# Two transformer blocks in split fp32 on one core: value projections in 512 columns, one modulation batch divided, and the head of the second block's layers reordered

## The reference

```python
for i in range(2):                                    # first block
    sh1, sc1, g1, sh2, sc2, g2 = split(silu_c @ ada_w[i] + ada_b[i], 6)
    h, hc = rmsnorm(x) * (1 + sc1) + sh1, rmsnorm(xc) * (1 + csc1) + csh1
    q, k, v = split(concat(h, hc) @ wqkv, 3)          # i = 0: differential attention, 8 heads
    x = x + g1 * (attend(q, k, v) @ wo)               # i = 1: neighbourhood attention, 16 heads
    x = x + g2 * (gated(conv(norm_mod(x, sc2, sh2) @ w_up)) @ w_down)
for l in range(2):                                    # second block
    p = rmsnorm(x) @ w_in                             # q, kv, gates, fox q/k/v, fox f, ...
    kc, vc = compress(k_c), compress(v_c)             # flat @ w1, silu, @ w2
    logf = log_sigmoid(fox_f + bias); c = cumsum(logf)
    x = x + merged(nsa, pool, conv, fox) @ w_out
```

## Time and profile before

| what | value |
|---|---|
| median of three runs | 1661.72 us (1661.22 to 1662.11) |
| profiled execution | 1660.64 us, its span 1658.5 us |
| TensorE busy, share of the span | 1606.6 us, 97% |
| VectorE, ScalarE, GpSimd busy | 54%, 45%, 33% |
| mean granted TensorE clock | 0.987 |

### The profile page before, as it was taken

One profiled execution on the slowest core, in us unless ns is written; L12 is line 12 of the kernel. 1 busy time (PEld: TensorE's weight loads), 2 busy tenths in 40 slices (PEclk: granted clock), 3 DMA queues, 4 the chain that ended last, 5 costly groups with the idle time before them and its releaser, 6 DMA issues.

```text
span 1658.5 us, 26678 instructions
## 1 busy us (share of the span) xinstructions
PE 1606.6 (97%) x10956; PEld 1404.6 (85%) x10956; DVE 890.6 (54%) x1406; ACT 749.2 (45%) x1359; POOL 545.7 (33%) x358
## 2 busy tenths in 40 slices
PE   7999988999999999999999999998999999999998
PEld 4779557778767888778968999998999999899998
DVE  4334584455524554342265888548575457668434
ACT  5223584444313443243375655445544444554443
POOL 2214253322202222121172111024423577423554
PEclk9999999999999999999999999999999999999999
DMA  9264601443255222357224454554435545533551
GB/s 395 82 254 156 229 1 52 153 155 143 86 187 187 94 78 79 136 203 230 99 54 155 148 184 155 175 174 147 161 123 174 179 149 172 178 128 127 178 195 60
DMA packets 52984, 249.39 MB, mean 150 GB/s; under 512 B 20608, under 2 KB 21760, under 8 KB 26368
## 3 DMA queue, kind: packets, MB, share of 16 engines
q1 hardware_dynamic: 44400, 244.42, 42.4%
q10 hardware_dynamic: 8464, 3.28, 1.0%
HBM read 246.63 MB, written 1.05 MB: 149 GB/s over the span
## 4 chain that ended last, share of the span: by engine, by line
PE 86%; DVE 6%; ACT 3%; issue 1%; DMA 1%; POOL 1%; ACTq 1%; SPq 0%; POOLq 0%; DVEq 0%
PE psq L528 17%; PE psq L529 17%; PE psq L530 17%; PE ps L528 6%; PE ps L529 6%; PE ps L530 6%; PE ps L541 2%; PE psq L883 2%; PE psq L884 1%; PE psq L885 1%; DVE WL L510 1%; PE ps L1304 1%; PE psq L2122 1%; PE ps L1293 1%; PE psq L1261 1%
## 5 line engine op out<-in xcount | busy, mean ns | idle before, releaser
L528 PE MATMUL psq<-NH,WH 128*128 128x256 f32 (+1 forms) x1640 | 519.8, 317 | 3.9 <-DVE NL L793 2.0
L510 DVE TENSOR_TENSOR WL<-RAW,WH 128x1024 fp32r<-128x1024 f32 (+3 forms) x264 | 320.2, 1237 | 368.4 <-ACT WH L500 368.2
L529 PE MATMUL psq<-NL,WH 128*128 128x256 f32 (+1 forms) x1640 | 513.4, 313 | 0.0
L530 PE MATMUL psq<-NH,WL 128*128 128x256 f32 (+1 forms) x1640 | 513.3, 313 | 0.0
L510 POOL TENSOR_TENSOR WL<-RAW,WH 128x1024 fp32r<-128x1024 f32 (+2 forms) x116 | 302.3, 2608 | 556.2 <-ACT WH L500 543.8
L500 ACT ACTIVATE WH<-RAW 128x1024 fp32r<-128x1024 f32 (+2 forms) x380 | 361.0, 1000 | 177.7 <-DMA RAW<-wstream 127.2
L528 PEld LDWEIGHTS psq<-NH,WH 128*128 128x128 f32 x1640 | 314.2, 192 | 33.4 <-issue 12.0
L530 PEld LDWEIGHTS psq<-NH,WL 128*128 128x128 f32 x1640 | 314.1, 192 | 18.1
L529 PEld LDWEIGHTS psq<-NL,WH 128*128 128x128 f32 x1640 | 314.3, 192 | 16.8
L528 PE MATMUL ps<-NH,WH 128*128 128x256 f32 (+1 forms) x376 | 124.6, 331 | 0.0
L529 PE MATMUL ps<-NL,WH 128*128 128x256 f32 (+1 forms) x376 | 123.5, 328 | 0.0
(11 more groups left out here) (349 smaller groups left out, 2845.8 us busy)
## 6 DMA issues: line engine op xcount, KB each, us to landing
RAW<-wstream SPq DMA_DIRECT2D x196, 1024.0 KB, 4.9
RAW<-wstream SPq DMA_DIRECT2D x32, 704.0 KB, 4.1
K<-first SPq DMA_DIRECT2D x4, 1024.0 KB, 16.7
X<-xin SPq DMA_DIRECT2D x2, 1024.0 KB, 6.2
V<-first SPq DMA_DIRECT2D x2, 1024.0 KB, 19.2
Q<-first SPq DMA_DIRECT2D x2, 1024.0 KB, 24.9
BR<-rpb ACTq DMA_DIRECT2D x8, 256.0 KB, 10.0
BR<-rpb SPq DMA_DIRECT2D x8, 256.0 KB, 8.5
```

The costliest lines, as they stand in the source:

```text
L510: e.tensor_tensor(WL[:, u % 3, a:z], RAW[:, v % 3, a:z], WH[:, u % 3, a:z].bitcast(F32), ALU.subtract).then_inc(w_lo_p if pool else w_lo_v, 1)
L528: e.matmul(o, lh, rh, start=start, stop=False)
L529: e.matmul(o, lh, rl, start=False, stop=False)
L530: return e.matmul(o, ll, rh, start=False, stop=stop)
```

## The change

1. The values are projected in two pairs of units, each unit four input tiles by 512 columns (`pe_values`): 12 matmuls of 512 columns for each of four token tiles, each token tile in a bank of its own; the sums of a pair stay in their four banks (0 to 3, then 4 to 7) over both units. ScalarE copies four banks after the second unit of each pair. The waits move with it: token tiles 0 and 2 of the first unit wait for the copies of the last query and key units, `pe_diff` waits for all V copies before `pe_ada(2, 0)`.
2. Batch 5 keeps parameter 4 alone, with four units of two input tiles by 1024 columns; parameter 5 becomes batch 6, whose units are loaded behind `up(1,0)` and `up(1,1)` and multiplied in `pe_wo` (two) and ahead of the first two `up` units (two) of layer 1, its transposes ahead of the sixth. `dve_ada_halves` adds the two partial sums. The split of `up(1,1)` comes behind the norm.
3. `pe_out_turn` runs at the end of its step, behind the score product.
4. In the head `vf` is projected right behind `kf`, the LF transposes run between the two `cmp` products; ScalarE splits `vf` and the first `cmp` unit ahead of the forget gate, and VectorE makes the low parts of `vf` and `FHL`, both rotations, the low part of the first `cmp` unit and `dve_out_gain` ahead of the LF additions.

The core of the diff (bookkeeping of the orders, shapes and weight packing, and renumbered waits are left out):

```diff
 UP_ADA = {("up", 0, 0): (0, 1, 2, 3), ("up", 0, 2): (4,), ("up", 0, 3): (5,), ("up", 0, 4): (6,), ("up", 0, 5): (7,)}
-QKV_ADA = {("qkv", 1, 4): (0, 1, 2, 3), ("qkv", 1, 6): (4,), ("qkv", 1, 7): (5,), ("qkv", 1, 0): (6,), ("qkv", 1, 1): (7,)}
+QKV_ADA = {("qkv", 1, 4): (0, 1, 2, 3)}
+LATE_ADA = {("up", 1, 0): (0, 1, 2), ("up", 1, 1): (3,)}
+def ada_units(b):
+    return 8 if b < 5 else 4
...
             for j in range(4):
-                mm = e.matmul(AB[32 * j:32 * j + 32, :], CB[:, k, :], RAW[:, v % 3, 512 * j:512 * j + 512],
-                              start=k == 0, stop=k == DT - 1)
+                c = k if b < 5 else 2 * k + j // 2
+                mm = e.matmul(AB[32 * j:32 * j + 32, :], CB[:, c, :], RAW[:, v % 3, 512 * j:512 * j + 512],
+                              start=k == 0, stop=k == ada_units(b) - 1)
...
         def act_ada_row(e, b):
-            e.wait_ge(gemm, product(("ada", b, DT - 1)))
+            e.wait_ge(gemm, product(("ada", b, ada_units(b) - 1)))
...
+        def dve_ada_halves(e, b):
+            t = 32 + 8 * (b - 5)
+            to = ADA[:, 1, t:t + 8, :].rearrange("p (c q) v -> p c q v", c=2)
+            part = AB[:, :].rearrange("p (q k c s) -> p k c q s", q=4, k=2, c=2)
+            bias = small_at("adab", 48 + t, 8).rearrange("p (c q) -> p c q", c=2).unsqueeze(3)
+            e.wait_ge(ada_fin, b)
+            e.tensor_tensor(to, part[:, 0, :, :, 0:2], bias.to_broadcast([P, 2, 4, 2]), ALU.add).then_inc(ada_half, 1)
+            e.wait_ge(ada_half, b - 4)
+            e.tensor_tensor(to, part[:, 1, :, :, 0:2], to, ALU.add).then_inc(ada_par, 1)
         def dve_ada(e, b):
+            if b >= 5:
+                dve_ada_halves(e, b)
+                return
...
             for i in range(4):
-                b = qk_slot(8 + i)
...
                     pe_ada_turn(e, 1)
-                if i < 3:
-                    e.wait_ge(qk_sb, qk_outputs_before(l, 8 + i - 2))
-                else:
-                    pe_last_values(e, l)
-                    continue
-                pe_tall(e, ("qkv", l, 8 + i), [bank[b], bank[b + 1]], 256, nothing)
+                pe_values(e, l, i)
+        def pe_values(e, l, i):
+            key, pr, kh = ("qkv", l, 8 + i), i // 2, i % 2
+            v, wh, wl = weights(key)
+            for t in range(4):
+                if i == 3:
+                    (pe_na_qk if l else pe_diff_qk)(e, t)
+                if i == 0 and t % 2 == 0:
+                    e.wait_ge(qk_sb, qk_outputs_before(l, 7 + t // 2))
+                if i == 2 and t == 3:
+                    e.wait_ge(ada_par, 5 if l else 1)
+                c = slice(t * P, t * P + P)
+                for k in range(4):
+                    if t == 0:
+                        wait_weights(e, v, k)
+                    kk = 4 * kh + k
+                    mm = mm3(e, bank[4 * pr + t], NH[:, kk, c], NL[:, kk, c], wh[:, k, :], wl[:, k, :], kk == 0, kk == 7)
+                if kh or t == 3:
+                    mm.then_inc(gemm, 1)
...
                 key = ("qkv", l, 8 + i)
-                b = qk_slot(8 + i)
-                for q in range(2):
-                    if i == 3:
-                        (act_na_exp if l else act_diff_exp)(e, q)
-                    e.wait_ge(gemm, product(key, q))
-                    e.activation(V[l][:, 2 * q:2 * q + 2, 256 * i:256 * i + 256], pair(bank[b + q]),
+                for t in range(4 if i % 2 else 0):
+                    if i == 3 and t < 2:
+                        (act_na_exp if l else act_diff_exp)(e, t)
+                    e.wait_ge(gemm, product(key, t))
+                    e.activation(V[l][:, t, 256 * (i - 1):256 * (i - 1) + 512], bank[4 * (i // 2) + t],
...
                     h, qt, k0, nk = diff_job(j)
-                    if age == 11 and qt == 3 and h < 7:
-                        pe_out_turn(e, h)
...
                         pe_diff_qk(e, j)
+                j = n - 11
+                if 0 <= j < 28 and diff_job(j)[1] == 3:
+                    pe_out_turn(e, j // 4)
+                if n == 2:
+                    e.wait_ge(v_sb, 8)
...
                     e.wait_ge(att_pt, PT1 + 2 * p + 2)
+                    if p == 0:
+                        e.wait_ge(v_sb, 16)
...
                         pe_sums(e, n, m)
-            if l == 0:
-                pe_ada(e, 3, 0)
+            pe_ada(e, 6 if l else 3, 0)
...
                 pe_ada(e, 3, 2)
+            else:
+                pe_ada(e, 6, 1)
...
             for i in range(4):
-                split_hi(e, ahead(("wo", l, i)))
+                if (l, i) != (1, 3):
+                    split_hi(e, ahead(("wo", l, i)))
...
                         pe_ada_turn(e, 4)
+                    if l == 1 and j < 2:
+                        pe_ada(e, 6, 2 + j)
+                    if l == 1 and j == 6:
+                        pe_ada_turn(e, 6)
...
                         dve_ada(e, 3 + c)
+                    if l == 1 and jj == 6:
+                        dve_ada(e, 6)
...
             pe_raw_head(e, l)
-            for name in ("vn", "qf", "kf"):
+            for name in ("vn", "qf", "kf", "vf"):
                 pe_proj(e, l, name)
-            e.wait_ge(fx_v, FXV * l + 7)
-            for q in range(2):
-                mm = e.transpose(bank[3][:, q * P:q * P + P], LF[:, q, :], IDENT)
-            mm.then_inc(fx_tr, 1)
-            pe_proj(e, l, "vf")
...
             act_plain(e, l, "vn", VN[:, :, :])
+            act_plain(e, l, "qf", QF[:, :, :], 0.125)
+            for kind in range(2):
+                if kind == 0:
+                    e.wait_ge(flat, 5 * l + 5)
+                f = FLT[:, kind, :].rearrange("p (k n) -> p k n", k=16)
+                e.activation(FHV[:, kind, :, 0, :], f, ACT.Copy).then_inc(flat_hi, 1)
+            split_hi(e, ahead(unit_key(l, "kf")))
...
             e.activation(GS, VN[:, :, 128:140], ACT.Tanh, scale=0.5).then_inc(gs_a, 1)
-            act_plain(e, l, "qf", QF[:, :, :], 0.125)
-            for kind in range(2):
-                if kind == 0:
-                    e.wait_ge(flat, 5 * l + 5)
-                f = FLT[:, kind, :].rearrange("p (k n) -> p k n", k=16)
-                e.activation(FHV[:, kind, :, 0, :], f, ACT.Copy).then_inc(flat_hi, 1)
-            act_plain(e, l, "kf", KF[:, :, :])
+            act_out_of(e, l, "kf", KF[:, :, :])
+            act_plain(e, l, "vf", VF[:, :, :])
+        def act_decay(e, l):
...
                              bias=const_at("rows", 3 * a + 2)).then_inc(fx_a, 1)
-            act_plain(e, l, "vf", VF[:, :, :])
...
             e.memset(LF[:, :, :].bitcast(U32), 0).then_inc(fx_v, 1)
+            lo_prep(e, l, "qf", False)
             dve_turn(e, l, 0, QN[:, :, :])
+            for kind in range(2):
+                f = FLT[:, kind, :].rearrange("p (k n) -> p k n", k=16)
+                e.wait_ge(flat_hi, 2 * l + kind + 1)
+                e.tensor_tensor(FHV[:, kind, :, 1, :], f, FHV[:, kind, :, 0, :].bitcast(F32),
+                                ALU.subtract).then_inc(flat_lo, 1)
+            e.memset(CM[:, 0:384].bitcast(U32), 0).then_inc(cm_zero, 1)
+            dve_turn(e, l, 1, KN[:, :, :])
+            lo_prep(e, l, "kf", False)
+            if l == 0:
+                dve_out_gain(e, 5, "nout")
...
             e.tensor_scalar(GS, GS, 0.5, 0.5, ALU.mult, ALU.add).then_inc(gs_v, 1)
-            for kind in range(2):
-                f = FLT[:, kind, :].rearrange("p (k n) -> p k n", k=16)
-                e.wait_ge(flat_hi, 2 * l + kind + 1)
-                e.tensor_tensor(FHV[:, kind, :, 1, :], f, FHV[:, kind, :, 0, :].bitcast(F32),
-                                ALU.subtract).then_inc(flat_lo, 1)
-            e.memset(CM[:, 0:384].bitcast(U32), 0).then_inc(cm_zero, 1)
-            lo_prep(e, l, "qf", False)
-            dve_turn(e, l, 1, KN[:, :, :])
-            lo_prep(e, l, "kf", False)
-            if l == 0:
-                dve_out_gain(e, 5, "nout")
+            lo_prep(e, l, "vf", False)
+        def dve_decay(e, l):
...
                 mm.then_inc(gemm, 1)
+                if kind == 0:
+                    e.wait_ge(fx_v, FXV * l + 7)
+                    for q in range(2):
+                        mm = e.transpose(bank[3][:, q * P:q * P + P], LF[:, q, :], IDENT)
+                    mm.then_inc(fx_tr, 1)
...
                              ACT.Copy).then_inc(sb_copy, 1)
+                if kind == 0:
+                    act_decay(e, l)
...
                 split_lo(e, ahead(("cmp", l, kind)), pool)
+                if not pool and kind == 0:
+                    dve_decay(e, l)
```

More of the change, by code:

```diff
@@ L189, in unit_orders @@
         add(("qkv", 1, i), 1000)
[L190 to L195, removed]
+        if i == 5:
+            for k in range(ada_units(5)):
+                add_ada(5, k)
     for i in range(8, 12):
@@ L201, in unit_orders @@
         add(("up", 1, j), 1000)
+        for k in {0: (0, 1, 2), 1: (3,)}.get(j, ()):
+            add_ada(6, k)
     for m in range(DT):
@@ L222, in unit_orders @@
```

(36 more changed lines are left out.)

11 lines of the change are left out of this document (5 added, 6 removed).

## The result

The changed kernel takes 1646.54 us (median of four runs, 1643.65 to 1651.31) against 1661.47 for the kernel before (four runs): ratio 0.9918, interval 0.9889 to 0.9947. It is faster by 14.9 us where 23.8 were forecast; the time lies inside the range, near the case "the heads hand their wait on" (1646). The profiled execution is the longest of the four, 1651.31 us, span 1649.2.

A forecast was written before the change was run, and what follows sets the result against it. The prediction took TensorE's matmul stream as the bound, busy 1606.6 of 1658.5 us. Its terms summed to -23.8 against 1660.64, giving 1636.8, or 1637.9 with the median 1.1 above; range from 1632 with 2 us for the value stage's bounds to 1648.

The forecast's parts named there:

- the heads hand their wait on: Rival: in the hybrid heads vf's wait moves to cmp, FHL or the gain, half of 17.0 left: 1646; chance 0.16.
- Value projections: Value stages of both layers: 192 matmuls of 512 columns replace 384 of 256, 2.4 us less a layer.
- The wait in layer 0: Layer 0 value stage: third token tile of unit 8 waits 2.5 us for key copies, plus 1.5 for the clock.
- The last V copy: Ahead of pe_ada(2, 0): TensorE waits for the last V copy, +0.5 us (0 to 0.7).
- The output turn: Differential attention loop: the turn's wait of 1.20 goes but is given back through VectorE's scaling, -0.2 us (0 to -6.0).
- Batch 5: Layer 1: query and key stage -5.8 us from four units and a bias hole gone; ahead of the feed-forward net -0.5.
- The head of hybrid layer 0: Next projection starts 8.9 us earlier despite a 0.9 cmp hole, and 1.9 less for low clock: -10.8 us.
- the clock falls behind the cmp hole: Hybrid layer 0's head: +3.2 us, within the rival of new holes and the clock, 1642, chance 0.20.
- The head of hybrid layer 1: vf starts without its wait, and transposes and cmp end at 1430.75 instead of 1436.95: -6.2 us.
- The signs of being wrong: Layer 0's head: next projection starting later than 14 us behind vf; or the value stage showing a clock under 1.
- The value stage on four banks: Rival: cycling four banks drops the clock to 1.2 GHz, 1665 at 140 matmuls; nearly all of slower's 0.04 chance.
- the case with a low-clock stretch left: Head of hybrid layer 0: alternative to the -10.8 us if a low-clock stretch remains, given as -7.6.

The follow-up runs named there:

- the mended kernel: Changed kernel with last key unit's copies ahead of the split, low half of kf ahead of the flattening, both rotations behind everything else: 1631.53 us, again 1632.02.
- copies first: Changed kernel with ScalarE copying layer 0's last key unit out before the split that waits for a weight load: 1643.33 us.
- the old values: Value projections as before, four units of 256 columns, all else as in the kernel of 1631.53 us: 1637.55 us.
- the old turn: Output turn ahead of the score product again, all else as in the kernel of 1631.53 us: 1633.28 us.
- the second rotation alone: Changed kernel with only VectorE's second rotation in the hybrid heads moved behind everything else: 1636.14 us.
- the low half of kf alone: Changed kernel with only VectorE's low half of kf moved ahead of the flattening in the hybrid heads: 1654.94 us.

## Why the prediction was partly right

*Value projections.* Right. Layer 1 gained 2.7 (2.4 forecast), layer 0 without its new hole 2.36. The Trainium skill's fixed 2.5 ns a matmul (TensorE: Matmul & The Clock Gate, section "Wait — 56ns, not 53.3ns?") doesn't account for it: by it a layer would have gained 0.5, and undoing this part alone cost 5.5 us, of which the low clock in that profile explains some 1.7.

*The wait in layer 0.* Right in place and size: 2.35 for 2.5, released by the copy that was named, and gone when ScalarE's order is turned. The 1.5 for the clock behind it was there in one profile and not in the other.

*The last V copy.* Right: 0.69 us at `pe_ada(2, 0)`.

*The output turn.* Right: a little, a period of 9.97 instead of 10.06, and by the path that was named. VectorE's scaling waits 1.31 us for the turn, and the maximum behind it begins 2.1 us after the score product (238.10 against 236.01), where 2.0 was forecast. The score product now waits where the turn did (0.64 and 0.35 of the next period), for ScalarE:

```profile
236.01 1.13 PE L1123 MATMUL psq<-K,Q 64*128 64x512 f32 x4 [0.64 <-ACT PP L1174]
237.07 0.66 PE L1103 MATMUL ps<-CONST,TMP 128*128 128x128 f32 x4
...
241.02 0.70 PE L1123 MATMUL psq<-K,Q 64*128 64x512 f32 x2 [0.35 <-ACT TMP L1174]
```

```profile
237.83 0.35 DVE L1228 TENSOR_SCALAR TMP<-ps,STAT 128x128 f32<-128x128 f32 x1 [1.31 <-PE ps L1103]
238.10 1.21 DVE L1212 TENSOR_REDUCE STAT<-psq 128x2 f32<-128x1024 f32 x1
```

*Batch 5.* Right. The bias issue takes 5.46 us at 760.28 (12.57 before), there is no hole behind it, and the stage is 6.3 shorter. Ahead of the feed-forward net the hole for the norm is 0.81 instead of 1.81, and the clock stays at 1.00, as taken; the stretch from the values to the hybrid head is 0.8 shorter, for 0.5.

```profile
760.28 5.46 ACTq L1284 DMA_DIRECT2D BR<-rpb  x4
```

```profile
908.61 0.36 PE L911 MATMUL psq<-NH,WH 128*128 128x256 f32 x1 [0.81 <-DVE NL L821]
```

*The head of hybrid layer 0.* Wrong, and this is the step that failed: "VectorE runs behind 1139.5 a rotation (2.2) ... I take 0.9", and with it "-1.9 if the low clock goes with the hole of 4.80". Three things were off. VectorE's list was priced without what GpSimd does at the same time: the earlier split of vf put GpSimd's half on top of VectorE's half of kf, a hole of 1.27 that no rival named. The output gain ended 25.8 us behind the head's start (1147.91 - 1122.10) where 23.6 were taken (1150.7 - 1127.1). 1.8 of this is the wait in kf's low half; in the list behind it the rotation's 2.76 instead of 0.69 is nearly made up by the FHL lows, 0.75 instead of 2.23. So the cmp hole was 1.51 for 0.9, a small miss; but it was priced at its own length, and it brought the low clock, which the forecast saw leave with the old hole. A head without holes and at full clock takes 36.2 us (layer 1 of the mended kernel), so of 47.08 there are 1.27 + 1.51 of holes and 47.08 - 36.2 - 2.8 = 8.1 of low clock. These are the 10.2 us by which the term was off (1.27, 0.6 and 8.1). The rival "the clock falls behind the cmp hole" had the mechanism with 3.2 for the price.

The trace of before held a sign of it. Behind the hole of 4.80 the clock was back at 1.00 by 1155; it fell again from 1164.3 to 1171.2, 2.7 us behind a hole of 0.78 ahead of the cmp products, and this second stretch is what slowed the next projection. In the old head of layer 1, with a hole of 3.55 and none ahead of cmp, no second stretch came. The 1.9 that were to leave with the hole of 4.80 stood behind the cmp hole:

```profile
1161.67 0.33 PE L1922 MATMUL ps<-WH,FHL 128*128 128x128 f32 x1 [0.78 <-DVE WL L510]
```

```profile
1155.00:1160.00 5.00, 5.00 (x46) 5.00 (x45) 3.93 (x9) 2.49 (x5) 0.00 (x0) 1.00 0.45 187
...
1165.00:1171.00 6.00, 6.00 (x30) 6.00 (x30) 4.38 (x2) 3.00 (x4) 5.64 (x3) 0.50 0.94 325
```

*The head of hybrid layer 1.* The mechanism was right, the size not: -3.9 for -6.2. Holes of 1.26 ahead of kf and 0.64 ahead of cmp are 1.9 of the 2.3; no low clock there.

*The signs of being wrong.* Both came. The next projection of layer 0's head starts 20.4 us behind the start of vf (1160.98 - 1140.58) and 14.5 behind its end, where 14 was the limit, and the value stage of layer 0 shows a clock of 0.97, behind its hole.

*The rivals.* The value stage on four banks ran at 1.00 wherever it had no hole (layer 1 in both profiles; layer 0 with copies first), so that rival did not come up. That the time came out at the 1646 of "the heads hand their wait on" is in part luck. The wait did move on, to kf's low part and the gain (holes of 1.27, 1.51, 1.26 and 0.64), but the larger loss is the low clock, which that rival did not have; and the old head put back costs 6.1 us, not the 8.5 that were to be left.

*Small slips.* VectorE's list behind 1139.5 adds up to 1150.85, not 1150.7; the case with a low-clock stretch left is -7.5, not -7.6; and of the five turns alike in the loop four wait 1.2 and one 1.02, so that their end is -5.8.

What stays open is why the hole ahead of cmp brings the low clock so often. In the profiles of the new head and its variants it stood behind all seven holes of 1.45 to 3.45 us there, and behind none of 0.62, 0.64 and 1.25. But the length of the hole does not settle it: in the old head holes of 0.78 and 0.69 ahead of cmp were followed by some 7 us of it, a hole of 0.7 ahead of the next projection by 3.4 in two runs (the old values, the old turn) and by none in three, and holes of 2.31 to 2.45 elsewhere brought it in some profiles and not in others. The executions of 1636 to 1637 us with copies first make it likely that even a cmp hole of 1.5 does not always bring it. The products behind the cmp hole have 128 columns, those behind the other holes 256 or 512; no run changed them alone.

## What to carry to other kernels

Before work is moved earlier on one engine, lay the other engines' timelines beside it: the instruction that becomes early may fall on an older one that shares something with it. A hole on TensorE is not priced by its length alone: with the low clock behind it, 1.5 us cost 8 more here (in the profiled execution), and taking away a hole ahead of it made the kernel slower (1655) as long as the later one grew. Mend the last wait of a chain first; the second rotation alone gave 10 us, the low half of kf alone cost 9.

## What the runs showed of the hardware

GpSimd held VectorE up on these subtractions: VectorE's took 3.01 us with GpSimd's beside it, 1.22 without. It looks like a wait and not like a slowing: VectorE's instruction ended 1.08 us behind GpSimd's, about the 1.22 that it takes alone, and the rotation's product of 2.76 us ended 0.55 behind GpSimd's next one, about its 0.69 alone. The low part of FHL shows the same the other way: 2.23 us for the pair before, beside a half of GpSimd's from 1144.66 to 1147.01, and 0.75 after, at 1140.34, with GpSimd idle since 1139.15. The Trainium skill (SBUF — State Buffer, section "SBUF: two separate sides") says that a VectorE operation with two SBUF inputs and a GpSimd operation that reads SBUF share a port pair, that whichever starts first holds it for the whole instruction, and that the other is blocked meanwhile; the trace agrees, with the numbers above, GpSimd's having started first each time.

TensorE stayed at 0.50 for 13.7 to 17.1 us while it was busy almost without a break (17.07 of 17.07 us in the changed kernel), on the cmp products of 128 columns and the projection behind them. In the same products behind a hole of 0.64 (layer 1 of the changed kernel), or with none ahead (both heads with the second rotation late), it kept 1.00.
